# Value projections that stream two neighbouring weight blocks in one 512-column matmul

## The chip, the core and the metric

The kernel runs on one core of a Trainium2 chip. What counts is the device time of one execution in microseconds, as a median of runs.

## The reference

Three transformer layers on 256 tokens of width 1024, all in float32. The first mixes a gated convolution, a stick-breaking attention (16 heads of 64) and a cross attention to 256 memory tokens (4 heads of 256), and has a squared-ReLU feed-forward part. The other two each mix a forgetting attention ("fox", 8 heads of 64) with a retention (4 heads of 128) and have the same kind of feed-forward part. What bears on the change are the projections that make the values:

```python
# first layer
proj = h @ w_in                      # ... sv = 1024 columns
kv = mem_n @ w_mem_kv                # k, v = 1024 columns each
o_sb = stick_breaking_attention(to_heads(sq), to_heads(sk), to_heads(sv))
o = einsum("bhqk,bkhd->bqhd", p, v)  # memory cross attention
# second and third layer
proj = einsum('bsd,dc->bsc', x, w_in)
fq, fk, fv, f_logit, rq, rk, rv, rg = split(proj)   # fv, rv: 512 columns each
```

## The kernel before

All large weights come as blocks of 128 x 2048 float32 (1 MB): 1024 rows (8 tiles `k` of 128) by 256 output columns. SyncE loads block `l` into `raw[:, l % 2]` once the low part of block `l - 2` is made. ScalarE's `split` (L246 to L252) copies it to `w_hi[:, l % 4]` as float32r, VectorE's `split` (L616 to L621) subtracts and writes the low part `w_lo[:, l % 4]`. TensorE multiplies three times for each tile: high by high, high by low, low by high, all float32r. So raw has two slots and the split weights have a ring of four.

Most projections are `rows_first`: the weights are stationary (128 x 128) and the 256 tokens stream. Value projections are `tokens_first` (L1211): a tile of 128 tokens is stationary and the block's 256 weight columns stream, for `m` = 0, 1 (the two tiles of tokens). One block is 48 matmuls in either form. Each ends with an increment of `gemm_done`; the result is in bank `l % 3` of `gps`, from which ScalarE evacuates it (`evac`, L265), and block `l` may start when block `l - 3` is evacuated.

Value projections are blocks SV = 8 to 11 and MV = 28 to 31 of the first layer, and LFV = 6, 7 and LRV = 12, 13 of each of the other two, which one loop runs.

Each engine has its program written out by hand in one order and takes it in that order; semaphores tie them. On ScalarE a step `h` of the first layer is: evacuate block `h`; in even steps from SB0 = 10 on, stick-breaking work; `split(0, h + 4)`; from step 28 `head_squares(h - 28)`; from step 29 `head_rsqrt(h - 29)`; later the convolution's and the cross attention's work. On TensorE a step is the projection, then the attention work; from step 29 that is `head_sum(h - 29)`, which waits for `head_squares` of the same number and for the finished root (`hn_row`) of the number before, made by ScalarE's `head_rsqrt` and VectorE's Newton steps in `head_norm`.

In the loop of the other layers a step `l` on ScalarE is: evacuate block `l`; `split(h0, l + 4)`; in even steps from 8 on `fox_out((l - 8) // 2)`; `fox_copy(l - 6)`; `fox_exp(l - 5)`. On VectorE: `fox_out`, `fox_max(l - 5)`, `fox_scale(l - 5)`, from step 9 to 12 `rotate(l - 9)`, in step 13 the products with the decay, then the split of `l + 4`. On TensorE: the projection, `fox_values(l - 7)`, `fox_transpose(l - 6)`, `fox_scores(l - 5)`, `rotate(l - 9)`, and in step 13 the first three retention scores, which wait for the fourth rotation. The wait of ScalarE's split, which the change touches, is

```python
act.wait_ge(raw_loaded[raw_slot(l)], raw_count(h0, l))
if not start:
    act.wait_ge(s["gemm_done"], h0 + (l - 3))
```

Of the kernel before, what the change touches and what calls it, by code (L numbers as in the profile page):

```python
# [20 lines left out]
P = 128  # L21
D = 1024
T = 256
KT = D // P
# [50 lines left out]
def build(nc, mem_t, x_t, w1, w2, wf, par1, par2, con1, con2, out_t):  # L75
    with ExitStack() as ctx:
# [166 lines left out]
        def _(act):  # L243
            st = Steps(act, s["act_step"])

            def split(h0, l, n=HALF, start=False):  # L246

                act.wait_ge(raw_loaded[raw_slot(l)], raw_count(h0, l))
                if not start:
                    act.wait_ge(s["gemm_done"], h0 + (l - 3))  # L250
                act.activation(w_hi[:, ring(l), 0:n], raw[:, raw_slot(l), 0:n], ACT.Copy)\  # L251
                   .then_inc(s["hi_ready"], 1)  # L252

# [160 lines left out]
            for h in range(FFN1):  # L414
                ps = bank(h)
                if h < SK:
                    i = h - SQ
                    evac(qs[:, 2 * i:2 * i + 2, :], two(ps), h + 1, scale=0.125)
                elif h < SV:
                    i = h - SK  # L420
                    evac(ks[:, 2 * i:2 * i + 2, :], two(ps), h + 1)
                elif h < CC:
                    i = h - SV
                    evac(vs[:, :, 256 * i:256 * i + 256], two(ps), h + 1)
                elif h < CH:
                    i = h - CC
                    evac(u[:, 2 * i:2 * i + 2, 2:T + 2], two(ps), h + 1)
                elif h < MK:

                    if staged_n >= 2:  # L430
                        act.wait_ge(s["staged_free"], staged_n - 1)
                    evac(staged[:, staged_n % 2, :], ps, h + 1)
                    staged_n += 1
                elif h < MV or XQ <= h < XQ + 4:
                    i = h - (MK if h < MV else XQ)
                    evac((kx if h < MV else qx)[:, 2 * i:2 * i + 2, :], two(ps), h + 1)
                elif h < XQ:
                    i = h - MV
                    evac(vx[:, :, 256 * i:256 * i + 256], two(ps), h + 1)
                elif h < WO1:  # L440
                    if (h - 36) % 2 == 0:

                        act.wait_ge(s["gemm_done"], h + 1)
                        act.wait_ge(s["staged_free"], staged_n - 1)
                        act.activation(gate[:, staged_n % 2, :], ps, ACT.Sigmoid).then_inc(s["evac"], 1)
                    else:
                        act.wait_ge(s["staged_free"], staged_n - 1)
                        evac(staged[:, staged_n % 2, :], ps, h + 1)
                        staged_n += 1
                        if h > GATED["conv"]:  # L450
                            i = (h - GATED["conv"]) // 2
                            act.wait_ge(s["mg"], i + 1)
                            act.activation(Q_hi[:, 2 * i:2 * i + 2, :], merged[:, 2 * i:2 * i + 2, :],
                                           ACT.Copy).then_inc(s["mg_hi"], 1)
                else:
                    if h == WO1:
                        act.preload_act_table_set("natural_log_exp_and_others")
                    act.wait_ge(s["resid"], h - WO1 + 1)
                    squares(X, B5, h - WO1, h - WO1 + 1, s["nsq"])
                if h == MEM0:  # L460

                    act.wait_ge(s["mem_loaded"], 16)
                    for a in range(2):
                        squares(B7, B5, 2 * a, 2 * a + 2, s["nsq"])
                if h == MEM0 + 2:
                    rms_norm(1, B4, R_hi)
                if SB0 <= h <= SB0 + 18 and h % 2 == 0:
                    t = (h - SB0) // 2
                    if t >= 2:
                        sb_out(t - 2)  # L470
                    if t < SB_PAIRS:
                        sb_softplus(t)
                    if 1 <= t <= SB_PAIRS:
                        sb_exp(t - 1)
                if h + 4 < FFN1 + 2:
                    split(0, h + 4)
                if HN0 - 1 <= h < HN0 + 7:
                    head_squares(h - HN0 + 1)
                if HN0 <= h < HN0 + 8:
                    head_rsqrt(h - HN0)  # L480
                if XQ <= h < XQ + 4:

                    i = h - XQ
                    act.wait_ge(s["gemm_done"], XQ)
                    act.wait_ge(s["conv_y"], i + 1)
                    act.activation(R_hi[:, 2 * i:2 * i + 2, :], y[:, 2 * i:2 * i + 2, :], ACT.Copy)\
                       .then_inc(s["cv_hi"], 1)
                if h == XQ + 3:
                    act.wait_ge(s["cv_lo"], 4)
                x0 = XQ + 3  # L490
                if x0 + 2 <= h < x0 + 2 + X_HEADS:
                    cx_out(h - x0 - 2)
                if x0 + 1 <= h < x0 + 1 + X_HEADS:
                    cx_copy(h - x0 - 1)
                if x0 <= h < x0 + X_HEADS:
                    cx_exp(h - x0)
                if h == GATED["x"] - 1:
                    act.wait_ge(s["gemm_done"], h + 1)
                    for i in range(4):
                        act.activation(Q_hi[:, 2 * i:2 * i + 2, :], ox[:, 2 * i:2 * i + 2, :], ACT.Copy)\  # L500
                           .then_inc(s["ox_hi"], 1)
# [9 lines left out]
            with act.Fori(0, LAYERS) as ly:  # L511
# [30 lines left out]
                for l in range(LFFN):  # L542
# [9 lines left out]
                    elif l < LF:  # L552
                        evac(fq[:, 2 * a:2 * a + 2, :], two(ps), done, scale=0.125)
                    elif l < LFV:
                        evac(fk[:, 2 * a:2 * a + 2, :], two(ps), done)
                    elif l < LRQ:
                        evac(fv[:, :, 256 * a:256 * a + 256], two(ps), done)
                    elif l < LRK:
                        evac(rq[:, 2 * a:2 * a + 2, :], two(ps), done)
                    elif l < LRV:  # L560
                        evac(rk[:, 2 * a:2 * a + 2, :], two(ps), done, scale=P ** -0.5)
                    elif l < LRG:
                        evac(rv[:, :, 256 * a:256 * a + 256], two(ps), done)
                    elif l < LWO:
                        act.wait_ge(s["gemm_done"], done)
                        act.activation(rg[:, 2 * a:2 * a + 2, :], two(ps), ACT.Copy)
                        act.activation(rsig[:, 2 * a:2 * a + 2, :], two(ps), ACT.Sigmoid)\
                           .then_inc(s["evac"], 1)
# [2 lines left out]
                        act.activation(fgate[:, 0, :], gps[:, 3, 0:16], ACT.Copy).then_inc(s["f_gate"], 1)  # L571
                        fox_softplus()
                    if l + 4 < LWO + 3:
                        split(h0, l + 4)
                    if l >= 7 and l <= 14 and l % 2 == 0:
                        fox_out((l - 8) // 2)
                    if 6 <= l < 14:
# [597 lines left out]
        def _(pe):  # L1175
# [32 lines left out]
                        ins = rows_part(l, bank_, op_hi, op_lo, (nt,), range(KT))  # L1208
                ins.then_inc(s["gemm_done"], 1)

            def tokens_first(h0, l, bank_, op_hi, op_lo):  # L1211

                pe.wait_ge(s["lo_ready"], h0 + (l + 1))
                r = ring(l)
                for m in range(2):
                    for k in range(KT):
                        out = gps[:, bank_, m * 256:(m + 1) * 256]
                        wh, wl = w_hi[:, r, k * 256:(k + 1) * 256], w_lo[:, r, k * 256:(k + 1) * 256]
                        xh, xl = op_hi[:, k, m * P:(m + 1) * P], op_lo[:, k, m * P:(m + 1) * P]
                        pe.matmul(out, xh, wh, start=(k == 0), stop=False)  # L1220
                        pe.matmul(out, xh, wl, start=False, stop=False)  # L1221
                        ins = pe.matmul(out, xl, wh, start=False, stop=(k == KT - 1))  # L1222
                ins.then_inc(s["gemm_done"], 1)

            def sum_tiles(src, tiles, out, start, stop):
# [154 lines left out]
            for h in range(FFN1):  # L1380
# [4 lines left out]
                if h < SV:  # L1385
                    rows_first(0, h, h % 3, H_hi, H_lo, (s["nhi"], s["nlo"], 0) if h == 0 else None)
                elif h < CC:
                    tokens_first(0, h, h % 3, H_hi, H_lo)
                elif h < MK or XQ <= h < XQ + 4:
                    rows_first(0, h, h % 3, H_hi, H_lo)  # L1390
                elif h < MV:
                    rows_first(0, h, h % 3, R_hi, R_lo, (s["nhi"], s["nlo"], 4) if h == MK else None)
                elif h < XQ:
                    tokens_first(0, h, h % 3, R_hi, R_lo)
                elif h < WO1:
                    if (h - 36) % 2 == 0:
                        rows_first(0, h, h % 3, H_hi, H_lo)
# [48 lines left out]
            with pe.Fori(0, LAYERS) as ly:  # L1446
# [84 lines left out]
                for l in range(LFFN):  # L1531
# [18 lines left out]
                    elif l < LFV or LRQ <= l < LRV or LRG <= l < LWO:  # L1550
                        rows_first(h0, l, b, H_hi, H_lo, (s["nhi"], s["nlo"], ly * 8 + 12) if l == 0 else None)
                    elif l < LRG:
                        tokens_first(h0, l, b, H_hi, H_lo)
                    elif l == LWO + 3:
                        pe.wait_ge(s["lo_ready"], h0 + (l + 1))
                        rows_part(l, b, Q_hi, Q_lo, (0,), range(KT))
# [8 lines left out]
                        ins.then_inc(s["f_cols"], 1)  # L1565
                    if 7 <= l < 15:
                        if l == 7:
                            pe.wait_ge(s["evac"], e0 + LFV)
                        if l == 11:
                            pe.wait_ge(s["evac"], e0 + (LFV + 1))  # L1570
                        fox_values(l - 7)
                    if 6 <= l < 14:
# [138 lines left out]
```

## Time and profile before

| | |
|---|---|
| time, median of 3 runs | 1380.37 us (1379.97 to 1382.86) |
| profiled execution, first to last instruction | 1381.2 us |
| a further time of that execution | none is given on the page |
| TensorE busy | 1309.6 us, 10264 matmuls |
| VectorE busy | 808.1 us |
| ScalarE busy | 647.6 us |
| DMA | 214.58 MB, mean 155 GB/s |
| TensorE clock granted, mean | 0.984 |

Times are read from the start of the span. Busy shares of one engine overlap those of others; the duration of a matmul is modelled and longer than the distance between two starts, so the distance is what a matmul costs in a dense stretch. A plain float32 matmul is recorded as two.

### The profile page before, as it was taken

How to read it: one execution, taken by the hardware profiler on the slowest of the kernel's cores; microseconds unless marked ns; L12 is line 12 of the kernel's file. 1: busy time of each engine (PE TensorE's matmuls, PEld its weight loads, DVE VectorE, ACT ScalarE, POOL GpSimd, SP SyncE). 2: the span in 40 equal slices, each digit the busy share in tenths (PEclk: the TensorE clock that was granted, in tenths of full speed). 3: DMA queues.
4: the chain of work that ended last, by engine and by line, in shares of the span. 5: the costliest groups of instructions: out<-in, count | busy, mean ns of one | idle time of the engine just before them, and what ended most of it. 6: DMA issues, size and time to landing. Idle time of an engine off the chain costs nothing.

```text
span 1381.2 us, 24664 instructions
## 1 busy us (share of the span) xinstructions
PE 1309.6 (95%) x10264; PEld 1257.4 (91%) x10264; DVE 808.1 (59%) x905; ACT 647.6 (47%) x722; POOL 0.2 (0%) x4
## 2 busy tenths in 40 slices
PE   5999999999999999999999979999889997999994
PEld 5999999999998999999888879999888896999994
DVE  5666965745555745454565666454656657655555
ACT  4565555664443534343434445444254444544443
POOL 0000000000000000000000000000000000000000
PEclk9999999999999999999999999999999999999998
DMA  6653444444554454553523226555233321565550
GB/s 222 214 184 123 157 149 150 157 149 156 183 184 153 153 188 178 186 209 125 183 92 123 92 100 224 195 178 187 91 143 136 116 99 61 183 214 186 179 183 31
DMA packets 34354, 214.58 MB, mean 155 GB/s; under 512 B 4576, under 2 KB 8672, under 8 KB 8800
## 3 DMA queue, kind: packets, MB, share of 16 engines
q1 hardware_dynamic: 34272, 213.37, 43.7%
q8 instruction: 65, 1.06, 0.3%
q14 instruction: 17, 0.14, 0.0%
HBM read 212.31 MB, written 1.05 MB: 154 GB/s over the span
## 4 chain that ended last, share of the span: by engine, by line
PE 85%; DVE 6%; ACT 3%; issue 3%; DMA 2%; SPq 0%; DVEq 0%; ACTq 0%
PE gps L1182 50%; PE aps L1279 7%; PE aps L1277 7%; PE aps L1274 7%; PE gps L1220 2%; PE gps L1221 2%; PE gps L1222 2%; DMA raw<-w 2%; DVE w_lo L619 1%; PE aps L1315 1%; ACT w_hi L251 1%; PE aps L1462 1%; PE aps L1483 1%; PE gps L1228 1%; ACT B L304 1%
## 5 line engine op out<-in xcount | busy, mean ns | idle before, releaser
L619 DVE TENSOR_TENSOR w_lo<-raw,w_hi 128x2048 fp32r<-128x2048 f32 x204 | 454.1, 2229 | 285.9 <-ACT w_hi L251 285.5
L251 ACT ACTIVATE w_hi<-raw 128x2048 fp32r<-128x2048 f32 x204 | 378.5, 1857 | 231.9 <-PE aps L1279 123.9
L1182 PE MATMUL gps<-R_hi,w_hi 128*128 128x256 f32 x896 | 238.2, 287 | 18.7 <-ACT R_hi L309 11.8
L1182 PE MATMUL gps<-H_hi,w_hi 128*128 128x256 f32 x896 | 241.3, 291 | 12.6 <-ACT H_hi L309 5.9
L1182 PE MATMUL gps<-R_hi,w_lo 128*128 128x256 f32 x896 | 236.9, 286 | 0.0
L1182 PE MATMUL gps<-H_hi,w_lo 128*128 128x256 f32 x896 | 236.5, 285 | 0.0
L1274 PE MATMUL aps<-Q_hi,w_hi 128*128 128x256 f32 x768 | 217.7, 283 | 0.0
L1277 PE MATMUL aps<-Q_lo,w_hi 128*128 128x256 f32 x768 | 217.3, 283 | 0.0
L1279 PE MATMUL aps<-Q_hi,w_lo 128*128 128x256 f32 x768 | 217.3, 283 | 0.0
L1182 PEld LDWEIGHTS gps<-R_hi,w_hi 128*128 128x128 f32 x896 | 175.0, 195 | 20.5 <-ACT R_hi L309 12.6
L1182 PEld LDWEIGHTS gps<-H_hi,w_hi 128*128 128x128 f32 x896 | 174.2, 194 | 15.1 <-issue 7.4
L1182 PE MATMUL gps<-H_lo,w_hi 128*128 128x256 f32 x896 | 179.9, 285 | 0.0
L1182 PE MATMUL gps<-R_lo,w_hi 128*128 128x256 f32 x896 | 179.5, 285 | 0.0
L1182 PEld LDWEIGHTS gps<-H_hi,w_lo 128*128 128x128 f32 x896 | 174.3, 195 | 1.1 <-issue 1.0
L1182 PEld LDWEIGHTS gps<-R_hi,w_lo 128*128 128x128 f32 x896 | 174.9, 195 | 0.0
L1274 PEld LDWEIGHTS aps<-Q_hi,w_hi 128*128 128x128 f32 x768 | 147.4, 192 | 0.1
L1277 PEld LDWEIGHTS aps<-Q_lo,w_hi 128*128 128x128 f32 x768 | 147.4, 192 | 0.1
L1279 PEld LDWEIGHTS aps<-Q_hi,w_lo 128*128 128x128 f32 x768 | 147.4, 192 | 0.0
L1182 PEld LDWEIGHTS gps<-H_lo,w_hi 128*128 128x128 f32 x896 | 140.3, 194 | 0.0
L1182 PEld LDWEIGHTS gps<-R_lo,w_hi 128*128 128x128 f32 x896 | 140.3, 194 | 0.0
L1182 PE MATMUL gps<-Q_hi,w_hi 128*128 128x256 f32 x320 | 85.1, 292 | 3.1 <-ACT Q_hi L601 3.1
L317 ACT ACTIVATE staged<-gps 128x512 f32<-128x512 f32 x48 | 28.5, 594 | 115.0 <-PE gps L1182 115.0
(229 smaller groups left out, 1654.2 us busy)
## 6 DMA issues: line engine op xcount, KB each, us to landing
raw<-w SPq DMA_DIRECT2D x198, 1024.0 KB, 4.8
B<-x_t SPq DMA_DIRECT2D x2, 512.0 KB, 4.5
B<-mem_t SPq DMA_DIRECT2D x1, 1024.0 KB, 7.7
B<-x_t SPq DMA_DIRECT2D x1, 1024.0 KB, 7.8
B<-con SPq DMA_DIRECT2D x1, 1024.0 KB, 6.8
out_t<-B SPq DMA_DIRECT2D x1, 1024.0 KB, 4.4
cst<-con SPq DMA_DIRECT2D x1, 320.0 KB, 4.8
raw<-wf SPq DMA_DIRECT2D x6, 16.0 KB, 1.6
```

The source lines that it names most:

```text
L251: act.activation(w_hi[:, ring(l), 0:n], raw[:, raw_slot(l), 0:n], ACT.Copy)\
L304: ins = act.activation(X[:, k, :], B1[:, k, :], ACT.Identity, bias=lpar[:, b + k:b + k + 1], scale=lpar[:, g + k:g + k + 1])
L317: act.activation(staged[:, a, :], gps[:, 2 * par_ + a, :], ACT.Relu)\
L619: dve.tensor_tensor(w_lo[:, ring(l), 0:n], raw[:, raw_slot(l), 0:n], w_hi[:, ring(l), 0:n].bitcast(F32), ALU.subtract)\
L1182: return pe.matmul(gps[:, bank_, nt * T:(nt + 1) * T], w[:, r, c:c + P], op[:, k, :], start=start, stop=stop, skip_group_check=True)
L1220: pe.matmul(out, xh, wh, start=(k == 0), stop=False)
L1221: pe.matmul(out, xh, wl, start=False, stop=False)
L1222: ins = pe.matmul(out, xl, wh, start=False, stop=(k == KT - 1))
L1228: ins = pe.matmul(out, ones, src[:, k, 0:T], start=(start and k == tiles[0]), stop=(stop and k == tiles[-1]))
L1274: pe.matmul(out, w_hi[:, r, c:c + P], hh, start=(first and k == 0 and nt % 2 == 0), stop=False, skip_group_check=True)
L1277: pe.matmul(out, w_hi[:, r, c:c + P], hl, start=False, stop=False, skip_group_check=True)
L1279: ins = pe.matmul(out, w_lo[:, r, c:c + P], hh, start=False, stop=(last and k == 3 and nt % 2 == 1), skip_group_check=True)
```

## The change

`tokens_first` goes; `tokens_pair` takes its place. For a pair of blocks `l0`, `l0 + 1` it runs once with `m` = 0 and once with `m` = 1: one tile of 128 tokens is stationary and 256 columns of each block, 512 in all, stream from two neighbouring ring slots into the whole bank. A pair is 2 x 24 matmuls of 512 columns in place of 2 x 48 of 256. Both runs read both blocks, so the first waits for the second block's low part too, and ScalarE's split of block `l0 + 4`, which overwrites `l0` in the ring, waits for the second run. An evacuation now takes one tile of tokens by 512 columns, so `fox_values(0)` waits for both of the pair (LFV + 1) at once.

```diff
@@ -243,11 +243,12 @@
         def _(act):
             st = Steps(act, s["act_step"])
 
-            def split(h0, l, n=HALF, start=False):
+            def split(h0, l, n=HALF, start=False, paired=()):
 
                 act.wait_ge(raw_loaded[raw_slot(l)], raw_count(h0, l))
                 if not start:
-                    act.wait_ge(s["gemm_done"], h0 + (l - 3))
+                    held = l - 4 in paired
+                    act.wait_ge(s["gemm_done"], h0 + (l - 2 if held else l - 3))
                 act.activation(w_hi[:, ring(l), 0:n], raw[:, raw_slot(l), 0:n], ACT.Copy)\
                    .then_inc(s["hi_ready"], 1)
 
@@ -421,7 +422,7 @@
                     evac(ks[:, 2 * i:2 * i + 2, :], two(ps), h + 1)
                 elif h < CC:
                     i = h - SV
-                    evac(vs[:, :, 256 * i:256 * i + 256], two(ps), h + 1)
+                    evac(vs[:, i % 2, 512 * (i // 2):512 * (i // 2) + 512], ps, h + 1)
                 elif h < CH:
                     i = h - CC
                     evac(u[:, 2 * i:2 * i + 2, 2:T + 2], two(ps), h + 1)
@@ -436,7 +437,7 @@
                     evac((kx if h < MV else qx)[:, 2 * i:2 * i + 2, :], two(ps), h + 1)
                 elif h < XQ:
                     i = h - MV
-                    evac(vx[:, :, 256 * i:256 * i + 256], two(ps), h + 1)
+                    evac(vx[:, i % 2, 512 * (i // 2):512 * (i // 2) + 512], ps, h + 1)
                 elif h < WO1:
                     if (h - 36) % 2 == 0:
 
@@ -473,7 +474,7 @@
                     if 1 <= t <= SB_PAIRS:
                         sb_exp(t - 1)
                 if h + 4 < FFN1 + 2:
-                    split(0, h + 4)
+                    split(0, h + 4, paired=(SV, SV + 2, MV, MV + 2))
                 if HN0 - 1 <= h < HN0 + 7:
                     head_squares(h - HN0 + 1)
                 if HN0 <= h < HN0 + 8:
@@ -554,13 +555,13 @@
                     elif l < LFV:
                         evac(fk[:, 2 * a:2 * a + 2, :], two(ps), done)
                     elif l < LRQ:
-                        evac(fv[:, :, 256 * a:256 * a + 256], two(ps), done)
+                        evac(fv[:, a, :], ps, done)
                     elif l < LRK:
                         evac(rq[:, 2 * a:2 * a + 2, :], two(ps), done)
                     elif l < LRV:
                         evac(rk[:, 2 * a:2 * a + 2, :], two(ps), done, scale=P ** -0.5)
                     elif l < LRG:
-                        evac(rv[:, :, 256 * a:256 * a + 256], two(ps), done)
+                        evac(rv[:, a, :], ps, done)
                     elif l < LWO:
                         act.wait_ge(s["gemm_done"], done)
                         act.activation(rg[:, 2 * a:2 * a + 2, :], two(ps), ACT.Copy)
@@ -571,7 +572,7 @@
                         act.activation(fgate[:, 0, :], gps[:, 3, 0:16], ACT.Copy).then_inc(s["f_gate"], 1)
                         fox_softplus()
                     if l + 4 < LWO + 3:
-                        split(h0, l + 4)
+                        split(h0, l + 4, paired=(LFV, LRV))
                     if l >= 7 and l <= 14 and l % 2 == 0:
                         fox_out((l - 8) // 2)
                     if 6 <= l < 14:
@@ -1208,18 +1209,19 @@
                         ins = rows_part(l, bank_, op_hi, op_lo, (nt,), range(KT))
                 ins.then_inc(s["gemm_done"], 1)
 
-            def tokens_first(h0, l, bank_, op_hi, op_lo):
-
-                pe.wait_ge(s["lo_ready"], h0 + (l + 1))
-                r = ring(l)
-                for m in range(2):
-                    for k in range(KT):
-                        out = gps[:, bank_, m * 256:(m + 1) * 256]
-                        wh, wl = w_hi[:, r, k * 256:(k + 1) * 256], w_lo[:, r, k * 256:(k + 1) * 256]
-                        xh, xl = op_hi[:, k, m * P:(m + 1) * P], op_lo[:, k, m * P:(m + 1) * P]
-                        pe.matmul(out, xh, wh, start=(k == 0), stop=False)
-                        pe.matmul(out, xh, wl, start=False, stop=False)
-                        ins = pe.matmul(out, xl, wh, start=False, stop=(k == KT - 1))
+            def tokens_pair(h0, l, m, op_hi, op_lo):
+
+                l0 = l - m
+                pe.wait_ge(s["lo_ready"], h0 + (l0 + 2))
+                r = ring(l0)
+                out = gps[:, l % 3, :]
+                for k in range(KT):
+                    wh = w_hi[:, r:r + 2, k * 256:(k + 1) * 256]
+                    wl = w_lo[:, r:r + 2, k * 256:(k + 1) * 256]
+                    xh, xl = op_hi[:, k, m * P:(m + 1) * P], op_lo[:, k, m * P:(m + 1) * P]
+                    pe.matmul(out, xh, wh, start=(k == 0), stop=False)
+                    pe.matmul(out, xh, wl, start=False, stop=False)
+                    ins = pe.matmul(out, xl, wh, start=False, stop=(k == KT - 1))
                 ins.then_inc(s["gemm_done"], 1)
 
             def sum_tiles(src, tiles, out, start, stop):
@@ -1385,13 +1387,13 @@
                 if h < SV:
                     rows_first(0, h, h % 3, H_hi, H_lo, (s["nhi"], s["nlo"], 0) if h == 0 else None)
                 elif h < CC:
-                    tokens_first(0, h, h % 3, H_hi, H_lo)
+                    tokens_pair(0, h, h % 2, H_hi, H_lo)
                 elif h < MK or XQ <= h < XQ + 4:
                     rows_first(0, h, h % 3, H_hi, H_lo)
                 elif h < MV:
                     rows_first(0, h, h % 3, R_hi, R_lo, (s["nhi"], s["nlo"], 4) if h == MK else None)
                 elif h < XQ:
-                    tokens_first(0, h, h % 3, R_hi, R_lo)
+                    tokens_pair(0, h, h % 2, R_hi, R_lo)
                 elif h < WO1:
                     if (h - 36) % 2 == 0:
                         rows_first(0, h, h % 3, H_hi, H_lo)
@@ -1550,7 +1552,7 @@
                     elif l < LFV or LRQ <= l < LRV or LRG <= l < LWO:
                         rows_first(h0, l, b, H_hi, H_lo, (s["nhi"], s["nlo"], ly * 8 + 12) if l == 0 else None)
                     elif l < LRG:
-                        tokens_first(h0, l, b, H_hi, H_lo)
+                        tokens_pair(h0, l, l % 2, H_hi, H_lo)
                     elif l == LWO + 3:
                         pe.wait_ge(s["lo_ready"], h0 + (l + 1))
                         rows_part(l, b, Q_hi, Q_lo, (0,), range(KT))
@@ -1565,8 +1567,6 @@
                         ins.then_inc(s["f_cols"], 1)
                     if 7 <= l < 15:
                         if l == 7:
-                            pe.wait_ge(s["evac"], e0 + LFV)
-                        if l == 11:
                             pe.wait_ge(s["evac"], e0 + (LFV + 1))
                         fox_values(l - 7)
                     if 6 <= l < 14:
```

## Rows read from the trace of the kernel before

**Rows 1.** Page, part 1: busy us (share of the span) and instructions.
```profile
PE 1309.6 (95%) x10264; PEld 1257.4 (91%) x10264; DVE 808.1 (59%) x905; ACT 647.6 (47%) x722; POOL 0.2 (0%) x4
```

**Rows 2.** TensorE's list of waits: us in total, times, longest.
```profile
PE aps L1362 <- DVE B L869: 2.6, 2, 1.5
```

**Rows 3.** The chain that ended last: start us, us, what.
```profile
99.66 11.50 PE gps L1182 x96
...
245.47 4.84 DMA raw<-w
...
284.81 1.73 PE aps L1351 x8
```

**Rows 4.** Timeline of TensorE, a stretch at half clock: start us, us, what.
```profile
451.94 0.41 PE L1182 MATMUL gps<-R_hi,w_lo 128*128 128x256 f32 x1
...
452.58 0.41 PE L1182 MATMUL gps<-R_hi,w_hi 128*128 128x256 f32 x1
```

**Rows 5.** Timeline of TensorE, narrow matmuls of the forget gates.
```profile
650.74 0.28 PE L1546 MATMUL gps<-H_hi,w_hi 128*8 128x256 f32 x1
...
653.41 0.28 PE L1548 MATMUL gps<-H_hi,w_lo 128*8 128x256 f32 x1
...
659.37 0.61 PE L1563 MATMUL gps<-cst,soft 8*128 8x8 f32 x4
```

**Rows 6.** Groups by shape: busy us, mean ns, idle before.
```profile
L1220 PE MATMUL gps<-w_hi,H_hi 128*128 128x256 f32 x192 | 56.9, 296 | 0.0
```

**Rows 7.** Timeline of VectorE, splits of blocks 10 and 11.
```profile
72.58 4.58 DVE L619 TENSOR_TENSOR w_lo<-raw,w_hi 128x2048 fp32r<-128x2048 f32 x2 [0.97 <-ACT w_hi L251]
```

**Rows 8.** Timeline of ScalarE, step 29.
```profile
223.33 1.91 ACT L251 ACTIVATE w_hi<-raw 128x2048 fp32r<-128x2048 f32 x1
225.13 0.62 ACT L378 ACTIVATE sqh<-B 128x512 f32<-128x512 f32 x1
225.65 0.41 ACT L271 ACTIVATE rs<-rs 128x256 f32<-128x256 f32 x1
```

**Rows 9.** Timeline of VectorE, steps 29 and 30.
```profile
227.53 0.42 DVE L640 SCALAR_TENSOR_TENSOR rs<-rs 128x256 f32<-128x256 f32 x1
...
235.40 2.29 DVE L619 TENSOR_TENSOR w_lo<-raw,w_hi 128x2048 fp32r<-128x2048 f32 x1
```

**Rows 10.** Timeline of ScalarE, steps 6 and 7, second layer.
```profile
677.03 1.90 ACT L251 ACTIVATE w_hi<-raw 128x2048 fp32r<-128x2048 f32 x1
678.84 0.48 ACT L531 ACTIVATE spb<-aps 128x384 f32<-128x384 f32 x1
680.63 0.40 ACT L536 ACTIVATE spb<-spb,small 128x128 f32<-128x128 f32 x1 [1.31 <-DVE small L1026]
...
681.43 0.19 ACT L536 ACTIVATION_READ_ACCUMULATOR spb<-spb,small 128x1 f32 x1
684.95 0.60 ACT L267 ACTIVATE B<-gps 128x512 f32<-128x512 f32 x1 [3.33 <-PE gps L1222]
```

**Rows 11.** Timeline of ScalarE, step 12, second layer.
```profile
736.54 0.38 ACT L527 ACTIVATE Q_hi<-aps 128x256 fp32r<-128x256 f32 x1
```

**Rows 12.** Timeline of VectorE, step 12, second layer.
```profile
736.95 0.43 DVE L1041 TENSOR_TENSOR Q_lo<-aps,Q_hi 128x256 fp32r<-128x256 f32 x1 [1.97 <-ACT Q_hi L527]
737.84 0.56 DVE L1020 TENSOR_TENSOR spb<-aps,B 128x384 f32<-128x384 f32 x1 [0.47 <-PE aps L1465]
...
742.29 0.69 DVE L1051 TENSOR_TENSOR B<-B 128x512 f32<-128x512 f32 x1
```

**Rows 13.** Timeline of TensorE, step 13, second layer.
```profile
744.35 0.65 PE L1483 MATMUL aps<-spb,B 128*64 128x256 f32 x2
...
747.27 0.38 PE L1592 MATMUL gps<-B 128*128 128x128 f32 x2
```

**Rows 14.** Windows: us, busy of five engines, granted clock, DMA share, GB/s.
```profile
446.00:450.00 4.00, 0.62 (x3) 0.19 (x2) 2.23 (x6) 0.83 (x2) 0.00 (x0) 1.00 0.00 0
450.00:456.80 6.80, 5.64 (x26) 5.67 (x27) 5.60 (x12) 4.72 (x6) 0.00 (x0) 0.50 0.00 0
```

## The prediction, made before the changed kernel was run

> **What bounds the kernel now.** I read the page first, then TensorE's list of waits, the chain of waits, the groups by shape, and last the timelines of ScalarE, VectorE and TensorE where value projections stand. TensorE is busy for 95% of the span [rows 1], so a nanosecond saved per matmul is worth having, and a wait put in front of TensorE is paid in full. In the stretches that matter it hardly waits: in cross attention's head norms only for two transposes, 2.6 us in all [rows 2]. The chain runs for long pieces through TensorE alone [rows 3]; between 223 and 285 us it runs through ScalarE's splits, head-norm steps, VectorE's splits and the weight loads (one load of it in [rows 3]), although TensorE works there nearly all the time: two loops of about equal length.
>
> **What the matmuls gain.** 96 projections of 256 columns take 11.50 us, 119.8 ns each [rows 3]. Their streaming is not what costs that. At half clock they start 213 ns apart (451.94 to 452.58 is three steps) [rows 4], which is 256 columns at 1.2 GHz with nothing over; at full clock streaming alone would be 106.7 ns. Matmuls with 8 stationary columns still step by 116 ns (650.74 to 653.41, 23 steps), and with 8 moving columns by 118 ns ((0.61 - 0.26) / 3) [rows 5]: there is a floor of some 118 ns for a weight load with its matmul, whatever their width. The nearest row for a longer stream is the plain float32 matmul of 256 columns, 1.73 us for 8, 216.2 ns each [rows 3]: that is 2 x 106.7 ns plus 3, with its weight load hidden. 512 float32r columns are as long a stream, so I take 216.2 ns in place of 2 x 119.8: 23.4 ns saved for each of 384 pairs (16 weight blocks of 48 matmuls; 192 of the first kind in [rows 6] are 12 of the blocks), 9.0 us in all. Bounds: 239.6 ns, twice the present step, saves nothing; 213.3 saves 10.1 us; if the 13.1 ns above 106.7 is an addition for each instruction, 5.0 us.
>
> The Trainium skill (TensorE: Matmul & The Clock Gate, Back-to-back issue gap) gives a matmul N/2.4 + 2.5 ns: 109.2 for 256 columns, 215.8 for 512. By that rule the change saves only 2 x 109.2 - 215.8 = 2.6 ns a pair, 1.0 us in all. The trace disagrees on 256 columns (119.8), and agrees with the rule's shape only for the longer stream.
>
> **What the new waits cost.** The rest is the edit in ScalarE's split. The split of the block four after a pair's first now waits for the matmuls of the pair's *second* block. ScalarE takes its program in order, so everything written behind that split waits too: a whole projection (5.2 us) plus the split. What counts is what stands behind it and how soon TensorE asks for it.
>
> *Blocks 8 to 11 (SV).* Behind the split stand evacuations and softplus(0), which TensorE needs a projection later or more; the splits of 12 and 13 wait for their loads anyway. Block 11's low part, now needed before block 10 starts, is ready at 72.58 + 4.58 = 77.16 us [rows 7], block 10 would start at 77.25. No loss; gain 96 x 23.4 = 2.25 us.
>
> *Blocks 28 to 31 (MV).* Behind split(32) stands head_squares(0), for which TensorE's head_sum(0) waits right after projection 29. From the end of projection 29: wake-up 0.1, split 1.80 (223.33 to 225.13), squares 0.6 [rows 8]: TensorE stands 2.5 us. Behind split(34) stand head_squares(2) and head_rsqrt(1); head_sum(2) wants both, the second through VectorE's Newton steps. From the end of projection 31: 0.1 + 1.80 + 0.52 (225.13 to 225.65) + 2.30 (225.65 to the end of the step at 227.53) + 0.1 [rows 8, 9] = 4.85 us. Now the loop of ScalarE, VectorE and loads. Before, VectorE's split of block 34 began at 235.40 [rows 9]. After, counting from 210.1 where projection 28 starts: 5.2 + 0.8 (sb_values) + 5.2 + 2.5 + 0.9 + 5.2 + 0.9 + 5.2 + 4.8 + 0.9 (norm) = 31.6, so 241.7: 6.2 us later, the gain inside MV already in it. From there the loop repeats every 13.1 us (split 2.2, load 4.84 [rows 3], high part, squares, root, norm), as TensorE's two projections with head sums do (13.2), so nothing is won back, and TensorE's 2.6 us of slack only covers its own smaller delay. MV: +6.2 us.
>
> *Blocks 6, 7 (LFV), in each layer.* fox_values(0) after projection 7 now wants projection 7's own evacuation. ScalarE has split(10), fox_copy(0) and fox_exp(1) in front of it, all held until projection 7 ends: 0.1 + 1.81 (677.03 to 678.84) + 0.4 + 1.0 (680.63 to 681.6; its maximum is long there) + 0.60 + 0.1 [rows 10] = 4.0 us in which TensorE stands. Less 48 x 23.4 ns = 1.1: +2.9 us a layer.
>
> *Blocks 12, 13 (LRV), in each layer.* Behind split(16) stand fox_out(2), fox_copy(6), fox_exp(7). VectorE is blocked as well: its fox_out(2) waits for ScalarE's, and behind it stand fox_max(7), fox_scale(7), rotate(3). TensorE after projection 13 wants fox_values(6), transpose(7), then rotated keys for the retention scores. From the end of 13: split done 1.9; VectorE's Q_lo 0.41 later (736.54 to 736.95), which takes 0.43: fox_max(7) starts at 2.7. From fox_max's start to the start of the last step of rotate is 742.29 - 737.84 = 4.45, and 0.7 for that step: 7.85; adding wake-up, retention scores start at about 7.9 us. Three of them take 1.95 us, so TensorE gets on at 9.8, where it now does at 3.15 (744.35 to 747.27, and two steps of 0.11) [rows 11, 12, 13]. Added 6.65, less 1.1: +5.5 us a layer. What is next late (loads 18 and 19, split(17)) has a projection's time in hand.
>
> **The clock.** In 446 to 450 TensorE was nearly idle, then stood at half clock for 6.8 us [rows 14]. Half clock on 256-column work costs 213 against 120 ns, 3.0 us if the whole 6.8 us is worked through. LRV's 8 us with only 1.2 us of matmuls in it is the likeliest new place; part of the slow stretch then falls in the gap itself: I take 1.5 us a layer of 0 to 3. MV's gap is covered by the loop of VectorE; LFV's 4.0 us gap I count as nothing (0 to 2.9).
>
> **Sum.** -2.25 + 6.2 + 2 x 2.9 + 2 x 5.5 + 2 x 1.5 = +23.8 us. The profiled execution is 1381.2 us from first to last instruction; the page gives no other time for it. That is 0.8 above the median of the runs, so I add to the median: 1404.
>
> **Rivals.**
> *The held splits cost nothing (faster).* Were the held work all early enough, the matmul gain alone would be left: 1380.4 - 9.0 = 1371. For it: TensorE waits for almost nothing now, and ScalarE idles 3 to 4 us before most evacuations. Against: that idle time lies before the projection's end, the new hold begins after it. It decides only where the six gaps together stay under 9 us; they come to 2.5 + 4.85 + 2 x 4.0 + 2 x 6.65 = 28.7. Chance 0.03.
> *LRV is hidden.* If ScalarE's order does not block VectorE so long (all but 1 us of that stall is absent), 2 x (5.5 + 1.5) less 2 go: 1392. Chance 0.07.
> *No gain from 512 columns.* The row that could show a 512-column float32r matmul is missing. Then the stalls stay and 9.0 comes on top: 1413. Chance 0.08. By the Trainium skill's rule above, 8.0 would come on top: 1412, the same case.
> *Clock everywhere.* Every gap of 4 us brings a full slow stretch: 2 x 2.9 for LFV and 2 x 1.5 more for LRV: 1413. Chance 0.12.
> *No change.* Gains and losses meet within 0.2% (2.8 us), about what a measurement of this kernel can tell from nothing: it needs two of the three kinds of stall to fail. Chance 0.03.
> Forecast as told: 0.67.
>
> Range 1394 to 1413: up to both 1413 cases, down to just above the hidden LRV; the forecast's own range is 1399 to 1410. Faster 0.04, same 0.03, slower 0.93.
>
> **What would show it.** In the new profile: matmuls of 512 columns starting 216 ns apart; a wait of TensorE of 2.5 and one of 4.8 us before head sums; a wait of 4 us before fox_values(0) on ScalarE's evacuation; three waits after projection 13, in each layer, summing to 6 or 7 us, the last on VectorE's rotation; VectorE's split of block 34 some 6 us later; half clock after the longest gaps. I am wrong if ScalarE's queue behind a held split is done before TensorE asks, or if the 512-column step is not near 216.

## The result, and the profile after

The changed kernel takes 1423.07 us (median of 4 runs, 1421.15 to 1428.98) against 1380.38: a ratio of 1.0313, with an interval of 1.0290 to 1.0336. It is 42.7 us slower; 23.8 were forecast, and 1413 was the upper end. Its profiled execution spans 1422.9 us and took 1424.96, so here the time lies 2.1 us above the span.

The page of the changed kernel, its head and part 1 (busy us, share, instructions):

```profile
span 1422.9 us, 23890 instructions
...
PE 1324.1 (93%) x9880; PEld 1249.6 (88%) x9880; DVE 807.6 (57%) x905; ACT 647.2 (45%) x722; POOL 0.2 (0%) x4
```

384 matmuls are gone, and yet TensorE is busy for 14.5 us more than in [rows 1]: something makes its matmuls longer. TensorE's waits after (us in total, times, longest), those that [rows 2] and the rest of that view did not have or had shorter:

```profile
PE aps L1485 <- ACT B L268: 7.5, 2, 3.7
...
PE aps L1485 <- DVE Q_lo L1042: 5.6, 2, 2.8
PE gps L1343 <- DVE rs L641: 4.9, 1, 4.9
...
PE aps L1475 <- DVE spb L1037: 4.3, 2, 2.2
PE aps L1462 <- DVE soft L1013: 3.8, 2, 2.9
...
PE gps L1343 <- ACT sqh L379: 2.6, 1, 2.6
...
PE aps L1591 <- DVE B L1052: 2.0, 2, 1.0
```

All but L1462 are waits that were forecast. L1343 is head_sum: 2.6 us for the squares (forecast 2.5), 4.9 for the root (4.8). L1485 is fox_values: 3.7 us a layer for the evacuation (4.0), and after projection 13, 2.8 for VectorE's Q_lo, then 2.2 for the transpose (L1475) and 1.0 for the rotation (L1591), 6.0 in all (6.65). L1462 is the first of the fox scores; of its 3.8 us, 1.7 were there before. The new ones sum to 29 us.

ScalarE's and VectorE's timelines behind projection 31, which ends at 238.2 (start, length, what):

```profile
238.43 1.91 ACT L252 ACTIVATE w_hi<-raw 128x2048 fp32r<-128x2048 f32 x1 [5.81 <-PE gps L1224]
240.25 0.61 ACT L379 ACTIVATE sqh<-B 128x512 f32<-128x512 f32 x1
240.77 0.40 ACT L272 ACTIVATE rs<-rs 128x256 f32<-128x256 f32 x1
241.20 0.42 ACT L274 ACTIVATE rs<-rs 128x256 f32<-128x256 f32 x1
241.52 0.58 ACT L268 ACTIVATE B<-gps 128x512 f32<-128x512 f32 x1
```

```profile
241.72 0.43 DVE L637 SCALAR_TENSOR_TENSOR rs<-rs 128x256 f32<-128x256 f32 x1 [8.41 <-ACT rs L274]
...
242.64 0.42 DVE L641 SCALAR_TENSOR_TENSOR rs<-rs 128x256 f32<-128x256 f32 x1
...
243.90 2.28 DVE L620 TENSOR_TENSOR w_lo<-raw,w_hi 128x2048 fp32r<-128x2048 f32 x1
```

The split waits 5.81 us for TensorE, then everything behind it comes in its own time, with the intervals of [rows 8, 9]: 1.82 to the squares, 0.52 to the root, VectorE's third Newton step done at 243.06, and head_sum(2) starts at 243.21. VectorE's split of block 34 starts at 243.90, where it did at 235.40: 8.5 us later, and 6.2 were forecast.

What the prediction had small is in the windows around the new gaps (length, busy of TensorE, granted clock, DMA share, GB/s):

```profile
215.00:250.00 35.00, 27.54 (x121) 0.85 0.32 115
690.00:712.00 22.00, 18.27 (x102) 0.84 0.28 98
755.00:775.00 20.00, 13.97 (x74) 0.74 0.24 86
1050.00:1070.00 20.00, 17.14 (x90) 0.83 0.47 163
1075.00:1095.00 20.00, 16.27 (x87) 0.83 0.23 73
1142.00:1160.00 18.00, 12.07 (x62) 0.72 0.24 73
```

Five of them hold the gaps that were forecast; the fourth, 1050 to 1070, holds the 2.9 us wait of the fox scores. All six are at a mean clock of 0.72 to 0.85. As the clock has only its two levels, 2.4 and 1.2 GHz (full and half clock here), 0.85 over 35 us is 10.5 us at half clock; the six together have 52 us of it. A 256-column matmul takes 213 ns there in place of 120, so 7/16 of the time that TensorE works through at half clock is lost: up to 23 us, less what falls into the gaps.

The new matmul, by shape (busy us, mean ns of one), and its starts in the timeline:

```profile
L1222 PE MATMUL gps<-w_hi,H_hi 128*128 128x512 f32 x96 | 40.1, 418 | 0.0
```

```profile
229.11 0.39 PE L1222 MATMUL gps<-w_hi,R_hi 128*128 128x512 f32 x1
...
230.47 0.39 PE L1222 MATMUL gps<-w_hi,R_hi 128*128 128x512 f32 x1
```

Six steps in 1.36 us: 227 ns for 512 columns, where I had taken 216.2; two of 256 take 239.6.

### The profile page after: what moved, and what is told of

It reads as the page before. It is cut to its first block, busy times and chain, and to the rows that moved or that the text cites. A ratio compares the mean times of both kernels' runs of the same rounds, so it can differ in the third digit from the quotient of the medians.

```text
span 1422.9 us, 23890 instructions
## 1 busy us (share of the span) xinstructions
PE 1324.1 (93%) x9880; PEld 1249.6 (88%) x9880; DVE 807.6 (57%) x905; ACT 647.2 (45%) x722; POOL 0.2 (0%) x4
## 4 chain that ended last, share of the span: by engine, by line
PE 84%; DVE 6%; ACT 4%; issue 3%; DMA 2%; SPq 0%; DVEq 0%; ACTq 0%
PE gps L1183 49%; PE aps L1281 6%; PE aps L1276 6%; PE aps L1279 6%; PE gps L1222 2%; PE gps L1224 2%; PE gps L1223 2%; DMA raw<-w 2%; DVE w_lo L620 1%; ACT w_hi L252 1%; PE aps L1317 1%; PE aps L1464 1%; PE aps L1485 1%; PE gps L1230 1%; PE aps L1462 1%
## 5 line engine op out<-in xcount | busy, mean ns | idle before, releaser
L1183 PE MATMUL gps<-H_hi,w_hi 128*128 128x256 f32 x896 | 244.6, 294 | 12.8 <-ACT H_hi L287 6.0
L1183 PEld LDWEIGHTS gps<-R_hi,w_hi 128*128 128x128 f32 x896 | 175.3, 196 | 18.8 <-ACT R_hi L310 12.6
L1183 PE MATMUL gps<-Q_hi,w_lo 128*128 128x256 f32 x320 | 82.2, 283 | 0.0
```

The lines of the kernel that those rows point to most:

```text
L1183: return pe.matmul(gps[:, bank_, nt * T:(nt + 1) * T], w[:, r, c:c + P], op[:, k, :], start=start, stop=stop, skip_group_check=True)
```

## The experiments

**Discarded matmuls in the new gaps.** Everything waits as in the changed kernel, but TensorE stays busy.

```diff
+def fill(l, n):
+    for _ in range(n):
+        pe.matmul(gps[:, l % 3, 0:T], H_hi[:, 0, 0:P], H_hi[:, 0, :], start=True, stop=True)
 ...
+if h in (HN0, HN0 + 2):
+    pe.wait_ge(s["evac"], h - 1)
+    fill(h + 1, 20 or 39)            # before head_sum
 ...                                  # second and third layer, each behind its own wait
+    fill(l + 1, 32)                  # l == 7, before fox_values(0)
+    fill(l + 1, 22)                  # l == 13, before fox_values(6)
+    fill(l + 1, 19)                  # ... before fox_transpose(7)
+    fill(l + 1, 10)                  # ... before the retention scores
```

> The changed kernel with idle TensorE time filled: in front of each of the new waits TensorE runs discarded 256-column matmuls into the bank that the next projection overwrites (20 before head_sum(0), 39 before head_sum(2), 32 before fox_values(0), 22, 19 and 10 around the three waits after projection 13), 2.4 + 4.7 us once and 3.8 + 2.6 + 2.3 + 1.2 us a layer. The new waits of the changed kernel come to 29 us and the matmuls save 4.8 us, which leaves 17 us of the 42.7 us unexplained. Theory A (the clock falls to half after the gaps, and the projections behind them run slow): the fillers keep the clock up and cost nothing themselves, so 10 to 17 us less than the changed kernel, 1406 to 1413 us. Theory B (the missing time is the loop of splits and loads getting late): the fillers change nothing, 1423 us, or add up to 3 us.

1407.53 us (ratio 1.0188, 1.0169 to 1.0207): 15.5 us less than the changed kernel, although TensorE has 225 matmuls more, and no run of the one comes near a run of the other. (The text above has 17 us unexplained; 42.7 - 29 + 4.8 is 18.5.) The same windows:

```profile
215.00:250.00 35.00, 34.59 (x209) 1.00 0.34 120
690.00:712.00 22.00, 22.00 (x161) 1.00 0.27 97
755.00:775.00 20.00, 19.86 (x152) 1.00 0.31 107
1050.00:1070.00 20.00, 20.00 (x103) 0.92 0.33 118
1075.00:1095.00 20.00, 20.00 (x142) 1.00 0.35 133
1142.00:1160.00 18.00, 18.00 (x125) 1.00 0.37 137
```

The clock stays at full speed but for some 3 us, and the waits are the same length, now spent working: ScalarE's split behind projection 31 waits 5.81 us for TensorE here too. So theory A holds: most of the 15.5 us were lost to the clock. Not all of it need be the clock behind the forecast gaps. The late load of the changed kernel's profile (below), with its 2.1 us of waiting and 6.8 us at half clock, is missing here, and against the changed kernel's two fastest runs (1421.2) the fillers give back 13.6 us.

The last transpose of cross attention's head norms that waits shows what the first layer pays, first in the changed kernel, then with fillers:

```profile
293.52 0.66 PE L1364 MATMUL aps<-cst,B 128*128 128x128 f32 x4 [1.52 <-DVE B L870]
```

```profile
290.36 0.66 PE L1370 MATMUL aps<-cst,B 128*128 128x128 f32 x4 [1.53 <-DVE B L870]
```

Before, it comes at 284.15. Counted from the start of projection 28 (210.13 before, 209.07 changed, 209.38 with fillers) that is 74.0, 84.5 and 81.0 us: MV costs 7.0 us without the clock's fall and 3.5 us more with it.

**Wide matmul alone, in the changed order.** Each 512-column matmul as two of 256, all waits kept.

```diff
-wh = w_hi[:, r:r + 2, k * 256:(k + 1) * 256]
+for j in range(2):
+    out = gps[:, l % 3, j * 256:(j + 1) * 256]
+    ... wh = w_hi[:, r + j, k * 256:(k + 1) * 256]
```

> The changed kernel with every wait and order as it is, but each 512-column matmul as two of 256 columns. In the changed kernel's trace 512 columns step by 227 ns, two of 256 take 239.8 ns. If that is all the wide matmul gives, 384 x 12.8 ns = 4.9 us more: 1428 us. If the wide matmul gave the 9.0 us of the prediction, 1432 us; if it gives nothing, 1423 us.

1424.77 us (ratio 1.0315, 1.0297 to 1.0332). 1.7 us above the changed kernel, with intervals that overlap: it settles nothing. Where the slow stretches fall changes by itself: here the fox scores of the third layer wait 0.8 us instead of the 2.9 of the changed kernel's profile, where one load of 1 MB landed late (ScalarE's split at 1052.19 waited 5.52 us for it) and another slow stretch followed. Behind the 2.6 us gap before head_sum(0), too, this profile has no half clock. Behind the other gaps, which are as long as in the changed kernel, it has half clock with 256-column matmuls as well, so the wide matmul is not what lowers the clock. The worth of the wide matmul is asked again below, without such gaps.

**The order written anew.** Both splits of a pair come in the step of its second block, and the head's squares and root before them.

```diff
-if h + 4 < FFN1 + 2:
-    split(0, h + 4, paired=(SV, SV + 2, MV, MV + 2))
 head_squares(h - HN0 + 1)     # each in its own steps, as before
 head_rsqrt(h - HN0)
+if h in PAIRS1:
+    pass
+elif h + 4 < FFN1 + 2:
+    if h - 1 in PAIRS1:
+        split(0, h + 3, paired=PAIRS1)
+    split(0, h + 4)
```

The same in the loop of the other layers; VectorE's splits move to the same steps, there the first of the two ahead of fox_max.

> The changed kernel with the order on ScalarE and VectorE written anew: the two splits of a pair both come in the step of the pair's second block, behind its evacuation, and head_squares and head_rsqrt come before the splits, so nothing stands behind a held split that TensorE wants soon. Theory A (all of the loss is what stands behind the held splits, with the clock that falls because of it): 1380.4 - 4.9 from the matmuls + 2 x 0.8 for fox_values(0), which still waits for the evacuation just before it: 1377 us, with no slow clock but those of before. Theory B (holding ring slots longer makes the loads late whatever the order): 1385 us or more, with waits for low parts of the splits on TensorE.

1377.90 us (ratio 0.9980, 0.9966 to 0.9993), 45 us less than the changed kernel and 3.0 less than the kernel before. Its waits, in place of those shown of the changed kernel:

```profile
PE aps L1477 <- DVE soft L1026: 1.9, 2, 1.0
PE aps L1500 <- ACT B L269: 1.4, 2, 0.7
...
PE gps L1358 <- DVE rs L650: 0.4, 1, 0.4
PE gps L1237 <- DVE w_lo L629: 0.2, 1, 0.2
```

and the places of the gaps:

```profile
215.00:250.00 35.00, 35.00 (x212) 1.00 0.47 176
684.00:704.00 20.00, 20.00 (x142) 1.00 0.46 158
735.00:750.00 15.00, 15.00 (x99) 1.00 0.33 116
```

The largest new gap is 0.7 us a layer before fox_values(0), and these stretches are at full clock; the mean over the whole execution is 0.987, since the slow stretches behind the norms stay. The ring slots are held as long as in the changed kernel, and TensorE waits for low parts (w_lo) 3.3 us in all, as before the change: theory A again, theory B falls.

**Late fox_values(0).** In step 7 the transpose goes first.

```diff
 if l == 7:
+    fox_transpose(l - 6)
     pe.wait_ge(s["evac"], e0 + (LFV + 1))
 fox_values(l - 7)
-if 6 <= l < 14:
+if 6 <= l < 14 and l != 7:
     fox_transpose(l - 6)
```

> The reordered kernel, and in step 7 of each layer fox_transpose(1) goes before fox_values(0), so that less of the wait for projection 7's evacuation (0.7 us in each layer in the reordered kernel's trace) is bare. At most 1.4 us less than the reordered kernel: 1376.5 us. If the transposes are too short a cover (0.4 us), 1377.2 us.

1376.69 us (ratio 0.9977, 0.9967 to 0.9988), the fastest kernel of this study. Against the one before it, 1.2 us by medians whose intervals overlap; its trace has the wait at 0.4 us instead of 0.7 a layer.

**Wide matmul alone, without gaps.** The reordered kernel with two of 256 columns, the edit of the second experiment.

> The reordered kernel with each 512-column matmul as two of 256: the worth of the wide matmul alone, with no new stall around it. A step of 227 against 2 x 120 ns: 384 x 13 ns = 4.9 us more than the reordered kernel, 1382.8 us. If the gain of the wide matmul is hidden by another engine, the same 1377.9 us.

1382.36 us (ratio 1.0004, 0.9995 to 1.0013): 4.5 us above the reordered kernel, 4.9 expected. The two intervals only just do not meet (0.9993 and 0.9995), but the size agrees with the steps. This is the worth of the wide matmul: without it the new order only equals the kernel before.

**The step by itself.** 384 discarded float32r matmuls behind TensorE's last work.

```diff
+for rows in (128, 8):
+    for n in (512, 384, 256, 128):
+        for i in range(48):
+            pe.matmul(aps[0:rows, 1, 0:n], R_hi[:, i % 8, 0:rows], w_hi[:, 0:2, ...n // 2 each])
```

> The changed kernel with 384 discarded float32r matmuls after TensorE's last work: 48 each of 512, 384, 256 and 128 moving columns with 128 stationary columns, then the same with 8. Measures the step by itself. If a float32r matmul costs its stream plus a fixed 13 ns: 227, 173, 120 and 66 ns. If instead a floor of about 118 ns holds per weight load and matmul and streaming is otherwise plain (the prediction's view): 216, 163, 120, 118 ns. With 8 stationary columns about 4 ns less where the fixed part depends on the weight load.

By shape (stationary rows*columns, moving shape, count, busy us, mean ns of one):

```profile
L1620 PE MATMUL aps<-w_hi,R_hi 128*8 128x512 f32 x48 | 11.3, 394 | 0.0
...
L1620 PE MATMUL aps<-w_hi,R_hi 128*128 128x384 f32 x48 | 8.5, 335 | 0.0
L1620 PE MATMUL aps<-w_hi,R_hi 128*128 128x256 f32 x48 | 5.9, 283 | 0.0
L1620 PE MATMUL aps<-w_hi,R_hi 128*8 128x256 f32 x48 | 5.8, 279 | 0.0
L1620 PE MATMUL aps<-w_hi,R_hi 128*128 128x128 f32 x48 | 5.5, 274 | 0.0
L1620 PE MATMUL aps<-w_hi,R_hi 128*8 128x128 f32 x48 | 3.0, 223 | 0.0
```

Busy is 47 steps and one modelled duration, so the step is (busy - mean) / 47, to about 1 ns. With 128 stationary columns: 174, 120 and 111 ns for 384, 256 and 128 moving columns (the group of 512 began at half clock; its step is the 227 ns of the changed kernel's timeline). Down to 256 that is the stream at 2.4 GHz plus 13 ns, whatever the width. With 8 stationary columns 256 take 117 ns, but 128 take 59: there is no floor of 118 ns for the pair of instructions. With 128 stationary and 128 moving columns the step is 111 ns, 58 above the stream and 52 above the step with 8 stationary: so the load of 128 stationary columns sets it there, as far as this one width shows. At 256 moving columns the step is longer than that, 120 ns.

**One pair alone, all else as before the change.** Each kernel keeps `tokens_first` and the old evacuation for the other blocks, as here for MV:

```diff
-split(0, h + 4, paired=(SV, SV + 2, MV, MV + 2))
+split(0, h + 4, paired=(MV, MV + 2, ))
-tokens_pair(0, h, h % 2, H_hi, H_lo)         # SV; likewise LFV, LRV
+tokens_first(0, h, h % 3, H_hi, H_lo)
```

> Only blocks 8 to 11 (SV) in pairs. Both theories: nothing waits, 96 x 12.8 ns = 1.2 us saved: 1379.5 us. If the held split costs something here too, 1381 us or more.

> Only blocks 28 to 31 (MV) in pairs, all else as before the change. Theory A (the waits, their knock-on in the loop of splits and loads, and the clock falling behind them): in the changed kernel's trace cross attention's transpose came 10.5 us later relative to the start of these blocks, so 1391 us. Theory of the prediction (the clock costs nothing here because the loop of VectorE is the later one): 1380.9 + 6.2 + 0.6 for the smaller saving = 1388 us.

> Only blocks 6 and 7 (LFV) of both layers in pairs. Theory A (wait of 4.1 us, 0.6 us saved, and 3.0 us lost at half clock behind the gap, in each layer): 1380.7 + 2 x 6.5 = 1394 us. Theory of the prediction (a 4 us gap does not bring the clock down): 1380.7 + 2 x 3.5 = 1388 us.

> Only blocks 12 and 13 (LRV) of both layers in pairs. Theory A: 6.65 us of waits, 0.6 us saved, 3 us at half clock, in each layer: 1380.7 + 2 x 9.0 = 1399 us. Without any clock loss 1393 us.

| in pairs | time, us | ratio | against before | forecast for this part, with clock |
|---|---|---|---|---|
| SV | 1379.57 | 0.9993 (0.9984 to 1.0002) | -1.3 | -2.25 |
| MV | 1390.77 | 1.0077 (1.0062 to 1.0093) | +10.1 | +6.2 |
| LFV, both layers | 1396.26 | 1.0108 (1.0093 to 1.0124) | +15.4 | +5.8 |
| LRV, both layers | 1397.39 | 1.0120 (1.0104 to 1.0135) | +16.5 | +14.0 |

They sum to +40.7; all together is +42.7. SV's gain is within what can be told from nothing, but nothing is lost there. The profiled run of MV alone is the fastest of its four, 2 us below the others, and has half clock behind the second gap only. LRV alone waits 11.3 us and saves 1.2; the other 6.4 us stand against 3 forecast for the clock. LFV alone missed its forecast by 9.6 us. Its windows, first the gap, then two slow stretches:

```profile
684.00:688.00 4.00, 0.27 (x2) 1.00 0.00 0
688.70:695.50 6.80, 6.80 (x26) 0.50 0.42 157
1060.80:1070.90 10.10, 10.10 (x38) 0.50 0.30 105
```

Here a gap of 3.7 us (TensorE's list of waits) was enough: right behind it come 6.8 us at half clock, in the third layer 10.2, and TensorE works through them without a pause. 17.0 us x 7/16 is 7.4 of the 15.4. The gap costs 3.8 us (fox_values(0) starts 4.12 us behind the last matmul of projection 7, less that matmul's 0.23 and the 0.1 between them before) and the wide matmul gives back 0.6: 2 x (3.8 - 0.6) = 6.4. So 1.6 of the 15.4 stay open.

**Fillers behind the norms.** On the reordered kernel with late fox_values(0), to win the clock back where the kernel before loses it too.

```diff
+fill(34, H_hi)          # before the first feed-forward part
 ...
 layer_norm(ly * 2)
+fill(48, H_hi)
 layer_norm(ly * 2 + 1)
+fill(48, R_hi)
```

> The reordered kernel with late fox_values(0), and discarded matmuls in the idle time of TensorE behind the norms (34 before the first feed-forward part, 48 behind each layer norm), to use the lesson on the clock. The traces show half clock for 3.4 to 6.8 us around each of those four gaps, 1.5 to 2.5 us lost behind each: 6 to 10 us less than the kernel it is built on, 1367 to 1371 us. If the clock falls all the same, or the fillers stretch the gaps, 1377 us or more.

1378.54 us (ratio 0.9984, 0.9975 to 0.9993): the clock is up (mean 0.996), and yet nothing is won. By medians it is 1.9 us slower than without, but the intervals overlap. The same stage of both, from a norm's matmuls to the next norm's, first with fillers, then without:

```profile
784.41 1.13 PE L1251 MATMUL aps<-B,cst 128*128 128x256 f32 x4 [0.30 <-ACT B L279]
```

```profile
984.92 1.13 PE L1251 MATMUL aps<-B,cst 128*128 128x256 f32 x4 [0.39 <-ACT B L279]
```

```profile
786.24 1.13 PE L1245 MATMUL aps<-B,cst 128*128 128x256 f32 x4 [0.30 <-ACT B L279]
```

```profile
986.73 1.13 PE L1245 MATMUL aps<-B,cst 128*128 128x256 f32 x4 [0.39 <-ACT B L279]
```

200.51 and 200.49 us: the slow stretch there cost nothing. A projection behind the norm waits for VectorE's split in either kernel, 0.44 us without fillers and 1.24 with them:

```profile
804.87 0.39 PE L1198 MATMUL gps<-R_hi,w_hi 128*128 128x256 f32 x1 [1.24 <-DVE w_lo L629]
```

And at the loop's turn the fillers did harm. From the last of those norm matmuls to the third layer's first projection it is 13.5 us with them (984.92 to 998.40) and 11.5 without (986.73 to 998.22). TensorE then stood 2.3 us for nothing that the profile shows (issue), which the kernel without fillers does not do; why stays open. The clock was low behind it all the same:

```profile
788.00:800.00 12.00, 11.35 (x80) 10.36 (x80) 8.90 (x15) 5.67 (x11) 0.00 (x0) 1.00 0.00 0
996.00:1008.00 12.00, 7.56 (x43) 7.27 (x42) 5.10 (x7) 6.59 (x11) 0.00 (x0) 0.72 0.03 7
```

## Why the prediction was wrong

**Direction and mechanism: right.** The held splits make TensorE wait for what stands behind them. The waits forecast at 28.7 us came to 27 in the places named. Moving that work out from behind the splits takes away all of the loss, 45 us, though the ring slots are held as long.

**The clock: the step that failed.** I wrote: "I take 1.5 us a layer of 0 to 3" for LRV, "MV's gap is covered by the loop of VectorE", and "LFV's 4.0 us gap I count as nothing". That is 3 us in the sum; the fillers give back 15.5 (13.6 against the fastest runs). LFV lost 9.0 and not 0 (15.4 less the gaps and the gain; 7.4 of it are traced to the clock), LRV 6.4 and not 3. MV's two gaps both brought half clock in the changed kernel, the 2.6 us one as well; these are TensorE's starts behind it:

```profile
225.30 0.63 PE L1223 MATMUL gps<-w_lo,R_hi 128*128 128x512 f32 x1
...
227.44 0.63 PE L1222 MATMUL gps<-w_hi,R_hi 128*128 128x512 f32 x1
```

Five steps in 2.14 us, 428 ns each. MV alone cost 10.1 us; without the clock's fall it would have been about 7.0. The loop of VectorE did not cover that, since the projections and head sums, which feed the loop, run on TensorE themselves. Its split of block 34 came 8.5 us later and not 6.2. Counted from the start of projection 28 it is 9.6 us, of which the fillers take away 1.6; another 1.0 is the four projections at 227 ns a matmul and not 216. I had the row for it in [rows 14] and gave the case "clock everywhere" 0.12, and even that with full slow stretches at LFV and LRV only, none at MV.

**The wide matmul: half its size.** The sum had 23.4 ns a pair and 9.0 us; measured are 12.6 ns, 4.8 us by the steps and 4.5 us by the run without gaps. A step that is not near 216 ns was one of my two signs of being wrong. I took a floor of 118 ns from [rows 5] and the 216 ns from the plain float32 row; the widths show 13 ns on top of the stream at any width from 256 up. [rows 5] mixed two things: 116 ns were 256 moving columns and some 9 ns, and 118 ns, by the widths, most likely the load of 128 stationary columns. The bound "addition for each instruction, 5.0 us" was right. The half clock's 213 ns with nothing over misled me: the addition shows at full clock only. At half clock a 512-column step is 428 ns, twice 213, so there the wide matmul saves nothing. The Trainium skill's rule for a matmul by itself (TensorE: Matmul & The Clock Gate, Back-to-back issue gap), N/2.4 + 2.5 ns, misses both: 227 and 120 ns are measured here against 215.8 and 109.2. Its saving of 1.0 us was too small, mine too large.

**The sum again.** Waits 27 in the places forecast + 15.5 given back by the fillers - matmuls 4.8 = 37.7 of 42.7 us, and 5.0 stay open. The 2.1 us of the late load in the third layer, seen in the one profiled execution, are no term of their own: the kernel with fillers does not have them, so they may be in the 15.5. The costs measured one pair at a time leave 2.0 of the 42.7. How far the late load has a share was not tried.

**SV** went as told, by half the gain. The rivals of no stall and of a hidden LRV are out.

## What to carry to other kernels

When a wait is put in front of an instruction, go down its engine's program from there and price each thing that another engine asks for; what matters is not the instruction that waits but what stands behind it, and the cure can be its place alone (45 us here). Count a gap on TensorE with the slow stretch behind it: in this kernel some 1.5 to 4.5 us more for most gaps where the work behind is TensorE's own, and nothing in the one stage looked at where VectorE sets the pace. A longer moving operand saves a fixed cost for each instruction, here 13 ns for each two matmuls made one, some 5% of their time: worth having only if it costs no wait.

## What had not been expected of the hardware

A gap of 3.7 us before fox_values(0) is followed by 6.8 to 10.2 us at half clock, and in the changed kernel one of 2.6 us was followed by 3.4; in the profiles of MV alone and of the changed order with 256 columns the same gap of 2.6 us was not. In the kernel before (668.6 to 671.9) and in the one with fillers (1049.9 to 1053.3) 3.3 and 3.4 us at half clock follow the fox scores, which had waited only 0.9 us. So the length of the gap does not tell it alone. The float32r matmul of 512 columns starts every 227 ns at full clock and every 428 at half: the 13 ns that it has over its stream are gone at half clock. With 8 stationary columns, 512 moving ones step by 232 ns, no less than the 227 with 128: a narrower weight load does not make the wide matmul faster.
